# Attention preparation in four lanes instead of three, squares in PSUM, the root asked for in another place

## Chip, cores and metric

The kernel runs on 1 core of one Trainium2 chip. The metric is the device time in microseconds (us) of one execution. The engines are TensorE (PE; PEld is its weight loads), VectorE (DVE), ScalarE (ACT), GpSimd (POOL) and SyncE (SP), which issues most DMAs.

## What is computed

Two blocks in a row on 1024 tokens and 256 context tokens of width 1024. The first block has two layers with a multi-head latent attention (8 heads, 96 wide: 64 plain and 32 rotated), two convolution branches and an output product; the second block has scans and a mixture of 64 experts. What the change touches is the preparation of queries and keys in the first block:

```python
def mla_q(cq, q_norm_w, w_uq, q_head_norm_w, cos, sin):
    q = (rms_norm(cq, q_norm_w) @ w_uq).reshape(B, T, MLA_HEADS, MLA_QK)
    q = rms_norm(q, q_head_norm_w)
    if cos is not None:
        q = jnp.concatenate([q[..., :MLA_NOPE], apply_rope(q[..., MLA_NOPE:], cos, sin)], axis=-1)

def mla_kv(ckv, kr, kv_norm_w, w_ukv, k_head_norm_w, cos, sin):
    kv = (rms_norm(ckv, kv_norm_w) @ w_ukv).reshape(B, T, MLA_HEADS, MLA_NOPE + MLA_V)
    k_nope, v = kv[..., :MLA_NOPE], kv[..., MLA_NOPE:]
    k = rms_norm(jnp.concatenate([k_nope, k_rope], axis=-1), k_head_norm_w)
    ...
```

Keys are rotated as queries are; context tokens are not rotated. `rms_norm(x, w)` is `x * rsqrt(mean(x*x) + eps) * w`. All is float32.

## The kernel before, in words

The kernel is one hand-ordered program: each engine has its own queue, filled in program order, and semaphores tie them together. The first block's attention is in `attention(l, last)`, called once for each of the two layers. It has a preparation, then a gate (all engines wait until all is done and landed), then the attention proper (scores, softmax, products), which again ends the stage for everyone. So nothing of another stage runs beside the preparation, and nothing of the attention proper starts ahead of its end.

**The start of the preparation.** SyncE loads `cq`, `ckv`, `kr` and two weights. ScalarE squares `cq` and `ckv` (L1088, L1090). TensorE sums the squares with products against one column of ones (L1100, L1101), 30 of them in layer 0 and 26 in layer 1, all into bank 6. VectorE scales the weights (L1068, L1070) and lays the tables of the rotation (L1077, L1078), then turns the sums into variances (L1080, L1081); ScalarE takes the roots (L1092, L1093), VectorE the reciprocals (L1083, L1084): `rq` and `rkv`, one factor for each token.

**The rows.** A row is one tile of 128 tokens for the queries ("q") or for the keys and values ("k"). Layer 0 has 20 rows (10 tiles, q and k in turn), layer 1 has 18 (the two context tiles only as k). Row n goes through these steps:

- TensorE: the product into the two PSUM banks of its lane (L1118 for q: 8 matmul instructions, 384 columns wide; L1120 for k: 4, 512 wide). The bank must have been left by the last copy of the row that used the lane before (`out`).
- ScalarE: copies out of the banks into `qt_`, times `rq` or `rkv` (L1143, two for q; L1145 and L1146, four for k).
- ScalarE: squares of `qt_` into `sqt` (L1151, 768 elements a partition, in SBUF).
- VectorE: sum of the squares by head (L1176), times 1/96 plus eps (L1178).
- ScalarE: the root (L1154, 8 elements).
- VectorE: reciprocal (L1181), `qt_` times it (L1183, 768 elements), then the rotation: L1190, L1191, L1193, L1194, or only L1197 for the two context tiles. For a k row VectorE also lays the position part into `qt_` (L1173).
- TensorE: eight transposes into the same banks (L1129).
- ScalarE: two copies out into `QT` or `KTt` (L1161, `out`).

**The order of the queues.** Three lanes (`work`, lane n % 3) hold the rows in flight: `hs`, `qt_`, `sqt`, `tmpr` in SBUF, and two banks each. `staged` writes the queues: it walks time steps t, and at each step it lets every lane that has begun (row n begins at step 2n) go on to its next `yield`, the oldest first. So the number of `yield`s in `prep_tensor`, `prep_scalar` and `prep_vector` sets where an instruction stands in its engine's queue. In ScalarE's queue this gives, at step 2m: copies out of row m-2, root of row m-1, copies in of row m; at step 2m+1: squares of row m. In VectorE's: reciprocal and scaling of row m-1 and position of row m; then rotation of row m-1 and sums of row m. In TensorE's: transposes of row m-2, product of row m.

Of the kernel before, what the change touches and what calls it, by code (L numbers as in the profile page):

```python
# [9 lines left out]
ALU = mybir.AluOpType  # L10
# [259 lines left out]
def program(nc, A, B, out, ar, ps, sems, known, pe, dve, act, pool, sp):  # L270
# [744 lines left out]
    def attention(l, last):  # L1015
# [26 lines left out]
        assert o <= LIM, (o, LIM)  # L1042
# [20 lines left out]
        def vector(e):  # L1063
# [15 lines left out]
            e.wait_ge(*Tn.at("sums"))  # L1079
            e.tensor_scalar(rq[:, ti0:NT], bank(6)[:, ti0:NT], 1.0 / 256, 1e-6, ALU.mult, ALU.add).then_inc(Vn.hit(), 1)  # L1080
            e.tensor_scalar(rkv, bank(6)[:, 16:26], 1.0 / 128, 1e-6, ALU.mult, ALU.add).then_inc(Vn.hit("vars"), 1)  # L1081
            e.wait_ge(*Sn.at("roots"))
            e.reciprocal(rq[:, ti0:NT], rq[:, ti0:NT]).then_inc(Vn.hit(), 1)  # L1083
            e.reciprocal(rkv, rkv).then_inc(Vn.hit("scales"), 1)  # L1084

        def scalar(e):
# [4 lines left out]
            e.wait_ge(*Vn.at("vars"))  # L1091
            e.activation(rq[:, ti0:NT], rq[:, ti0:NT], ACT.Sqrt).then_inc(Sn.hit(), 1)  # L1092
            e.activation(rkv, rkv, ACT.Sqrt).then_inc(Sn.hit("roots"), 1)  # L1093

        def tensor(e):
            e.wait_ge(*Sn.at("squares"))
            for ti in range(NT):
                if P * ti >= c0:
                    for k in range(2):
                        e.matmul(bank(6)[:, ti:ti + 1], sqa[:, k, P * ti:P * ti + P], ones[:, 0:1], start=k == 0, stop=k == 1)  # L1100
                i = e.matmul(bank(6)[:, 16 + ti:17 + ti], sqa[:, 2, P * ti:P * ti + P], ones[:, 0:1], start=True, stop=True)  # L1101
            i.then_inc(Tn.hit("sums"), 1)

        sync(sp), vector(dve), scalar(act), tensor(pe)
        rows = [(ti, kind) for ti in range(NT) for kind in ("q", "k") if kind == "k" or P * ti >= c0]

        def prep_tensor(e, n):
# [3 lines left out]
            hs, tmpr, qt_, sqt, bk = work[n % 3]  # L1111
            e.wait_ge(*Vn.at("weights"))
            for g in range(2):
                if n >= 3:
                    e.wait_ge(*Sn.at("out", n - 3, g))
# [5 lines left out]
                op.then_inc(Tn.hit("mm", n, g), 1)  # L1121
            yield
# [2417 lines left out]
```

## Time and profile before

| | |
|---|---|
| median of 3 runs | 4926.18 us (4925.58 to 4941.12) |
| profiled execution | 4966.66 us, of it the span 4964.8 us |
| busy: TensorE / VectorE / ScalarE / GpSimd | 86% / 40% / 27% / 10% |
| preparation, layer 0 | from 497.46 to 622.66 us of the span |
| preparation, layer 1 | from 1511.87 to 1625.83 us of the span |

Each of these two stretches runs from the first square of the stage to the end of its last copy out. The shares of the first line of busy times are means over the whole program; what the change is worth is to be read in the two stretches. The column PEclk of the views by stretch is the clock that TensorE was granted: 0.50 is 1.2 GHz, 1.00 is 2.4 GHz.

### The profile page before, as it was taken

The page shows a single profiled execution, that of the slowest core. Times are in us where ns is not written, and L with a number is a line of the kernel's source. Part 1 is how long each engine was busy: PE and PEld are TensorE (multiplying, and loading weights), DVE is VectorE, ACT ScalarE, POOL GpSimd, SP SyncE. Part 2 cuts the span into 40 slices and gives each one's busy share as a digit, 9 for nine tenths or more (in the row PEclk, how much of TensorE's full clock was granted, in tenths as well). Part 3 has the DMA queues.
Part 4 walks back from the last instruction along what each step waited for, and adds up shares of the span by engine and source line. Part 5 has one row for each costly group of instructions (what it writes and reads, how often), then busy time and mean ns, then how long its engine had stood idle before and what let it go on. Part 6 is the DMA issues. An engine that isn't in the chain of part 4 may idle for free. (4 is left out here: it accounts for less than half of the span.)

```text
span 4964.8 us, 68829 instructions
## 1 busy us (share of the span) xinstructions
PE 4278.5 (86%) x28006; PEld 2476.6 (50%) x28006; DVE 2000.1 (40%) x4088; ACT 1344.0 (27%) x3101; POOL 517.7 (10%) x560
## 2 busy tenths in 40 slices
PE   5999799999997899999997745788788799999991
PEld 2454456644444565454556534677575344434340
DVE  1631556611714665221006667666355222222223
ACT  2111645511015554111014454333141111111111
POOL 0000000000000000000010001222003322322220
PEclk9999879999998999999997867998897899999995
DMA  5011000030110002412111030000303578999973
GB/s 187 21 61 53 18 18 14 18 140 20 56 52 33 14 14 104 172 48 72 43 64 39 1 99 1 3 3 3 110 1 144 215 253 289 310 332 337 333 254 123
DMA packets 152451, 505.37 MB, mean 102 GB/s; under 512 B 22609, under 2 KB 79554, under 8 KB 138690
## 3 DMA queue, kind: packets, MB, share of 16 engines
q1 hardware_dynamic: 114898, 379.89, 20.6%
q0 software_dynamic: 37232, 120.99, 8.8%
q8 instruction: 227, 3.72, 0.3%
q14 instruction: 94, 0.77, 0.1%
HBM read 402.42 MB, written 98.42 MB: 101 GB/s over the span
## 5 line engine op out<-in xcount | busy, mean ns | idle before, releaser
L697 PE MATMUL banks<-arena 128*128 128x512 f32 (+1 forms) x2928 | 1107.7, 540 | 16.1 <-DMA arena<-in_w_in 10.4
L697 PEld LDWEIGHTS banks<-arena 128*128 128x128 f32 x2928 | 559.0, 191 | 563.6 <-issue 522.8
L3125 PE MATMUL banks<-arena 128*32 128x512 f32 (+2 forms) x2896 | 561.2, 595 | 3.1 <-DMA arena<-in_experts 2.3
L884 PE MATMUL banks<-arena 128*128 128x256 f32 (+1 forms) x1152 | 379.9, 485 | 21.6 <-DMA arena<-y_d 14.3
L1248 PE MATMUL banks<-arena 96*128 96x512 f32 (+1 forms) x800 | 376.7, 554 | 11.8 <-ACT arena L1351 10.1
L3125 PEld LDWEIGHTS banks<-arena 128*32 128x32 f32 (+2 forms) x2896 | 198.4, 130 | 357.0 <-issue 354.3
L1298 DVE TENSOR_REDUCE arena<-banks 128x1 f32<-128x512 f32 (+1 forms) x400 | 238.1, 595 | 242.2 <-PE banks L1248 240.6
L884 PEld LDWEIGHTS banks<-arena 128*128 128x128 f32 x1152 | 223.2, 195 | 169.7 <-issue 149.8
L3144 PE MATMUL banks<-arena 128*32 128x512 f32 (+2 forms) x1448 | 286.4, 595 | 1.7 <-DVE arena L3174 1.2
L1256 PEld LDWEIGHTS banks<-arena 128*128 128x128 f32 x1312 | 171.4, 143 | 154.1 <-issue 123.3
L3092 POOL DMA_INDIRECT r_d<-arena x125 | 181.5, 1452 | 639.0 <-DVE arena L3174 531.5
L1351 ACT ACTIVATE arena<-banks,arena 128x512 f32<-128x512 f32 (+1 forms) x400 | 239.3, 606 | 16.0 <-DVE arena L1307 2.8
L3209 ACT ACTIVATE arena<-banks 128x256 f32<-128x256 f32 x79 | 30.4, 385 | 780.5 <-PE banks L3125 780.5
L3181 DVE SCALAR_TENSOR_TENSOR arena<-arena,banks 128x256 f32<-128x256 f32 x79 | 38.1, 482 | 493.6 <-ACT arena L3209 493.6
L1256 PE MATMUL banks<-arena 128*128 128x128 f32 x1312 | 213.6, 276 | 0.1
L1357 ACT ACTIVATE arena<-banks 128x256 f32<-128x256 f32 (+1 forms) x272 | 131.8, 484 | 288.9 <-PE banks L1256 288.7
L1269 PE MATMUL banks<-arena 128*64 128x128 f32 x2624 | 191.9, 283 | 17.5 <-DVE arena L1312 13.4
L896 DVE SCALAR_TENSOR_TENSOR arena<-banks,arena 128x256 f32<-128x256 f32 (+1 forms) x72 | 43.2, 600 | 375.5 <-PE banks L884 375.5
L715 ACT ACTIVATE arena<-banks 128x512 f32<-128x512 f32 (+1 forms) x94 | 51.4, 547 | 514.2 <-PE banks L697 514.2
L3174 DVE TENSOR_TENSOR arena<-banks,arena 128x1024 f32<-128x1024 f32 x79 | 96.8, 1226 | 225.5 <-PE banks L3144 225.5
L723 ACT ACTIVATE arena<-banks 128x512 f32<-128x512 f32 (+3 forms) x95 | 50.5, 532 | 465.6 <-PE banks L697 460.2
L804 DVE SCALAR_TENSOR_TENSOR arena<-arena 128x1296 f32<-128x1296 f32 (+1 forms) x120 | 171.2, 1427 | 4.3
(505 smaller groups left out, 5714.8 us busy)
## 6 DMA issues: line engine op xcount, KB each, us to landing
arena<-in_experts SPq DMA_DIRECT2D x64, 3072.0 KB, 12.9
arena<-in_ada_w SPq DMA_DIRECT2D x12, 2048.0 KB, 7.6
arena<-in_w_in SPq DMA_DIRECT2D x19, 1024.0 KB, 6.7
arena<-in_w_mod SPq DMA_DIRECT2D x8, 2048.0 KB, 18.3
arena<-in_w_in SPq DMA_DIRECT2D x7, 2048.0 KB, 9.3
arena<-in_w_out SPq DMA_DIRECT2D x6, 2048.0 KB, 13.0
arena<-in_w_mod SPq DMA_DIRECT2D x8, 1024.0 KB, 5.4
arena<-r_d SPq DMA_DIRECT2D x16, 512.0 KB, 5.4
```

The lines of the kernel that those rows point to most:

```text
L697: i = e.matmul(self.out_of(n), lhs, rhs, start=k == 0, stop=k == KT - 1)
L804: e.scalar_tensor_tensor(z[:, lo:hi], a[:, lo - 15 + j:hi - 15 + j], reg(cw + 2 * j + ft, 1), z[:, lo:hi], ALU.mult, ALU.add).then_inc(Vn. ...
L884: i = e.matmul(bank(n % 4)[:, 0:nn], w[:, q, :], H[:, q, t0:t0 + nn], start=q == 0, stop=q == KT - 1)
L1248: op = e.matmul(bank(q)[:, 0:P * jn], QT[:, h, P * ti:P * ti + P], KTt[:, h, P * j0:P * (j0 + jn)], start=True, stop=True)
L1256: op = e.transpose(bank(3 + q)[:, P * j:P * j + P], pr[n % 2][:, P * (j0 + j):P * (j0 + j) + P], ident)
L1269: op = e.matmul(b[64 * (h % 2):64 * (h % 2) + 64, 0:P], V[:, j, 64 * h:64 * h + 64], ptr[n % 4][:, P * j:P * j + P], start=j == 0, stop=j ...
L1298: e.tensor_reduce(c[:, q:q + 1], bank(q)[:, 0:P * jn], AX.X, ALU.max).then_inc(Vn.hit(), 1)
L1351: e.activation(pr[n % 2][:, P * j0:P * (j0 + jn)], bank(q)[:, 0:P * jn], ACT.Exp, bias=c[:, 3:4], scale=SM, accum_out=c[:, 4 + q:5 + q]).t ...
L1357: e.activation(ptr[n % 4][:, P * j0:P * (j0 + jn)], bank(3 + q)[:, 0:P * jn], ACT.Copy).then_inc(Sn.hit("turn", n, q), 1)
L3092: e.indirect_dma_start(r_d[i % 2], bass.IndirectOffsetOnAxis(ap=lists[rows.start][0:rows.stop - rows.start, q, 0:1].bitcast(U32), axis=0), ...
L3125: op = e.matmul(ABK[(q - q0) % 2][rows, :], xT[(q - q0) % 2][:, P * k:P * k + P][:, rows], weights[:, i % SLOTS, 512 * k:512 * k + 512], s ...
L3144: op = e.matmul(OBK[rows, 512 * n:512 * n + 512], hT[(q - q0) % 2][:, P * f:P * f + P][:, rows], weights[:, i % SLOTS, o:o + 512], start=f ...
```

## The change

Four lanes instead of three, each with two of the eight banks. Room for the fourth lane: the squares no longer have a place in SBUF but go into the first 384 columns of the lane's two banks (`squares`), from which the row's copies have been made by then, and the two halves of `tmpr` lie apart. The sum over each head (now L1197) reads PSUM. The token sums at the start are split into two groups of tiles (0 to 2 into bank 6, 3 to 9 into bank 7); the second group's work is written behind the product of row 0. In the rows, the root is one `yield` later, the copies out are one or two later, and VectorE's rotation follows the scaling without a `yield`. Cut to its core:

```diff
-        for i in range(3):
+        for i in range(4):
             hs = reg(o, 8); o += 8
             qt_ = reg(o, 768).rearrange("p (h n) -> p h n", h=HN); o += 768
-            sqt = reg(o, 768).rearrange("p (h n) -> p h n", h=HN)
-            tmpr = reg(o, 512).rearrange("p (a h n) -> p a h n", a=2, h=HN); o += 768
-            work.append((hs, tmpr, qt_, sqt, [bank(2 * i), bank(2 * i + 1)]))
+            tmpr = [reg(at, 256).rearrange("p (h n) -> p h n", h=HN) for at in (o, o + 256 if i < 3 else ST + 3840)]; o += 512 if i < 3 else 256
+            squares = ps[:, 1024 * i:1024 * i + 1024].rearrange("p (g n) -> p g n", g=2)[:, :, 0:384]
+            work.append((hs, tmpr, qt_, squares, [bank(2 * i), bank(2 * i + 1)]))
...
+        groups = [(0, 3, bank(6)), (3, NT, bank(7))]
+
+        def sums_tensor(e, g):
+            t0, t1, out = groups[g]
             e.wait_ge(*Sn.at("squares"))
+            for ti in range(t0, t1):
+                if ti >= ti0:
                     for k in range(2):
+                        op = e.matmul(out[:, ti:ti + 1], sqa[:, k, P * ti:P * ti + P], ones[:, 0:1], start=k == 0, stop=k == 1)
+                op = e.matmul(out[:, 16 + ti:17 + ti], sqa[:, 2, P * ti:P * ti + P], ones[:, 0:1], start=True, stop=True)
+            op.then_inc(Tn.hit("sums", g), 1)
+            yield
...
+        steps(sums_tensor(pe, 0)), steps(sums_vector(dve, 0)), steps(sums_scalar(act, 0))
...
         def prep_tensor(e, n):
...
-                if n >= 3:
-                    e.wait_ge(*Sn.at("out", n - 3, g))
+                if n >= 4:
+                    e.wait_ge(*Sn.at("out", n - 4, g))
+                elif n == 3:
+                    e.wait_ge(*Vn.at("vars", 1))
...
             yield
             yield
             yield
+            yield
             e.wait_ge(*Vn.at("turned", n))
...
         def prep_scalar(e, n):
...
             yield
-            e.wait_ge(*Sn.at("rows", n))
+            e.wait_ge(*Sn.own())
             if kind == "k":
                 e.wait_ge(*Vn.at("position", n))
-            e.activation(sqt, qt_, ACT.Square).then_inc(Sn.hit("sq", n), 1)
+            e.activation(squares, qt_.rearrange("p h n -> p (h n)").rearrange("p (g n) -> p g n", g=2), ACT.Square).then_inc(Sn.hit("sq", n), 1)
+            yield
             yield
             e.wait_ge(*Vn.at("var", n))
             e.activation(hs, hs, ACT.Sqrt).then_inc(Sn.hit("root", n), 1)
+            yield
             yield
             yield
             if n < 2:
...
         def prep_vector(e, n):
...
             e.wait_ge(*Sn.at("sq", n))
-            e.tensor_reduce(hs, sqt, AX.X, ALU.add).then_inc(Vn.hit(), 1)
+            e.tensor_reduce(hs.rearrange("p (g h) -> p g h", g=2), squares.rearrange("p g (h n) -> p g h n", h=4), AX.X, ALU.add).then_inc(Vn.hit(), 1)
             e.wait_ge(*Vn.own())
             e.tensor_scalar(hs, hs, 1.0 / QK, 1e-6, ALU.mult, ALU.add).then_inc(Vn.hit("var", n), 1)
+            yield
             yield
             e.wait_ge(*Sn.at("root", n))
             e.reciprocal(hs, hs).then_inc(Vn.hit(), 1)
             e.wait_ge(*Vn.own())
             e.tensor_tensor(qt_, qt_, hs.unsqueeze(2).broadcast_to([P, HN, QK]), ALU.mult).then_inc(Vn.hit("scaled", n), 1)
-            yield
             w32, cw, sw = turns[kind]
...
+        for e, lane, sums in ((pe, prep_tensor, sums_tensor), (dve, prep_vector, sums_vector), (act, prep_scalar, sums_scalar)):
+            staged((1, sums(e, 1)), *((2 * n, lane(e, n)) for n in range(len(rows))))
```

Two places show what this does to the queues. The first is ScalarE's queue in the rows of layer 0, from the copies out of an old row on; L1161 and, in the changed kernel, L1182 are copies out, L1154 and L1174 the root, L1143 and L1162 the copies in of a q row, L1145/L1146 and L1164/L1165 those of a k row, L1151 and L1170 the squares. Before:

```order
L1161 ACTIVATE arena<-banks,arena 96x4x128 x2
L1154 ACTIVATE arena<-arena 128x8
L1143 ACTIVATE arena<-banks,arena 128x384 x2
L1151 ACTIVATE arena<-arena 128x768
L1161 ACTIVATE arena<-banks,arena 96x4x128 x2
L1154 ACTIVATE arena<-arena 128x8
L1145 ACTIVATE arena<-banks,arena 128x4x64
L1146 ACTIVATE arena<-banks,arena 128x256
L1145 ACTIVATE arena<-banks,arena 128x4x64
L1146 ACTIVATE arena<-banks,arena 128x256
L1151 ACTIVATE arena<-arena 128x768
```

and the same place of the changed kernel:

```order
L1182 ACTIVATE arena<-banks,arena 96x4x128 x2
L1162 ACTIVATE arena<-banks,arena 128x384 x2
L1174 ACTIVATE arena<-arena 128x8
L1170 ACTIVATE banks<-arena 128x2x384
L1182 ACTIVATE arena<-banks,arena 96x4x128 x2
L1164 ACTIVATE arena<-banks,arena 128x4x64
L1165 ACTIVATE arena<-banks,arena 128x256
L1164 ACTIVATE arena<-banks,arena 128x4x64
L1165 ACTIVATE arena<-banks,arena 128x256
L1174 ACTIVATE arena<-arena 128x8
L1170 ACTIVATE banks<-arena 128x2x384
```

The root stood behind the copies out and ahead of the copies in; now it stands behind the copies in of the next row and right ahead of that row's squares, and the copies out belong to a row one further back.

The second is VectorE's queue around one row with rotation (L1183 and L1205 the scaling, L1176 and L1197 the sums of squares, L1173 and L1194 the position). Before, from the variance of one row to that of the next:

```order
L1178 TENSOR_SCALAR arena<-arena 128x8
L1181 RECIPROCAL arena<-arena 128x8
L1183 TENSOR_TENSOR arena<-arena 128x768
L1173 COPY arena<-arena 128x8x32
L1190 TENSOR_TENSOR arena<-arena 128x256
L1191 TENSOR_TENSOR arena<-arena 128x256
L1193 TENSOR_TENSOR arena<-arena 128x8x16
L1194 TENSOR_TENSOR arena<-arena 128x8x16
L1176 TENSOR_REDUCE arena<-arena 128x8
L1178 TENSOR_SCALAR arena<-arena 128x8
```

and the same place of the changed kernel:

```order
L1199 TENSOR_SCALAR arena<-arena 128x8
L1194 COPY arena<-arena 128x8x32
L1203 RECIPROCAL arena<-arena 128x8
L1205 TENSOR_TENSOR arena<-arena 128x768
L1211 TENSOR_TENSOR arena<-arena 128x256
L1212 TENSOR_TENSOR arena<-arena 128x256
L1214 TENSOR_TENSOR arena<-arena 128x8x16
L1215 TENSOR_TENSOR arena<-arena 128x8x16
L1197 TENSOR_REDUCE arena<-banks 128x8
L1199 TENSOR_SCALAR arena<-arena 128x8
```

The position copy moved ahead of the reciprocal, and the sums read the banks; the rest keeps its order. In TensorE's queue the product of row m now stands ahead of the transposes of row m-2, and in layer 0 21 of the 30 token sums stand behind the product of row 0.

## Rows read from the trace of the kernel before

**Rows 1.** Busy by stretch: length, PE, PEld, DVE, ACT, POOL, PEclk, DMA share, GB/s:

```profile
497.46:622.66 125.20, 89.22 (x340) 57.93 (x340) 71.97 (x173) 76.11 (x145) 0.00 (x0) 0.81 0.05 15
1511.87:1625.83 113.96, 81.36 (x300) 52.20 (x300) 66.57 (x163) 69.10 (x133) 0.00 (x0) 0.80 0.05 16
```

**Rows 2.** Waits from 520 to 620 us (us in total, times, longest):

```profile
PE banks L1129 <- DVE arena L1194: 23.1, 11, 3.0
...
DVE arena L1176 <- ACT arena L1151: 19.9, 12, 5.5
...
DVE arena L1181 <- ACT arena L1154: 14.9, 20, 1.8
```

**Rows 3.** Timeline in layer 0 (start us, us, engine, line, operation):

```profile
570.87 0.17 DVE L1178 TENSOR_SCALAR arena<-arena 128x8 f32<-128x8 f32 x1
571.08 0.21 ACT L1154 ACTIVATE arena<-arena 128x8 f32<-128x8 f32 x1
571.19 0.46 ACT L1145 ACTIVATE arena<-banks,arena 128x256 f32<-128x256 f32 x1
...
572.43 0.28 DVE L1173 COPY arena<-arena 128x256 f32<-128x256 f32 x1
...
572.81 0.84 ACT L1151 ACTIVATE arena<-arena 128x768 f32<-128x768 f32 x1
...
574.65 1.26 ACT L1161 ACTIVATE arena<-banks,arena 96x512 f32<-96x512 f32 x2 [1.00 <-PE banks L1129]
...
574.81 0.17 DVE L1178 TENSOR_SCALAR arena<-arena 128x8 f32<-128x8 f32 x1
...
575.81 0.20 ACT L1154 ACTIVATE arena<-arena 128x8 f32<-128x8 f32 x1
```

**Rows 4.** Roots by layer (first and last start), and two of them in the timeline:

```profile
L1154 ACT ACTIVATE arena<-arena x20: 196/202/211, 521.7 to 617.2; 128x8 f32<-128x8 f32 x20
...
L1154 ACT ACTIVATE arena<-arena x18: 195/201/210, 1532.8 to 1620.4; 128x8 f32<-128x8 f32 x18
...
538.49 0.21 ACT L1154 ACTIVATE arena<-arena 128x8 f32<-128x8 f32 x1
...
1542.86 0.21 ACT L1154 ACTIVATE arena<-arena 128x8 f32<-128x8 f32 x1
```

**Rows 5.** Timeline, products and transposes on TensorE:

```profile
513.89 5.05 PE L1118 MATMUL banks<-arena 128*128 128x384 f32 x8
...
563.32 1.94 PE L1129 MATMUL banks<-arena 128*96 128x128 f32 x8 [2.90 <-DVE arena L1194]
...
573.97 1.08 PE L1129 MATMUL banks<-arena 128*96 128x128 f32 x8 [2.48 <-DVE arena L1194]
574.89 2.75 PE L1118 MATMUL banks<-arena 128*128 128x384 f32 x8
...
1526.16 6.65 PE L1120 MATMUL banks<-arena 128*128 128x512 f32 x8
```

**Rows 6.** Busy time by stretch in layer 0 (PEclk is third from the end):

```profile
520.00:541.00 21.00, 13.58 (x58) 7.49 (x56) 14.40 (x30) 16.91 (x35) 0.00 (x0) 1.00 0.00 1
...
541.00:616.00 75.00, 54.22 (x203) 32.75 (x204) 51.11 (x123) 49.96 (x100) 0.00 (x0) 0.87 0.00 1
...
563.00:566.00 3.00, 2.69 (x10) 2.32 (x11) 1.29 (x4) 1.39 (x3) 0.00 (x0) 0.50 0.00 0
```

**Rows 7.** Groups by shape, whole span, VectorE: sums of 512, 256 and 768 elements:

```profile
L1298 DVE TENSOR_REDUCE arena<-banks 128x1 f32<-128x512 f32 x256 | 177.0, 691 | 212.6 <-PE banks L1248 211.1
...
L1298 DVE TENSOR_REDUCE arena<-banks 128x1 f32<-128x256 f32 x144 | 61.1, 424 | 29.6 <-PE banks L1248 29.6
...
L1176 DVE TENSOR_REDUCE arena<-arena 128x8 f32<-128x768 f32 x38 | 36.1, 949 | 36.6 <-ACT arena L1151 36.6
```

**Rows 8.** Layer 1: token sums on TensorE, and the last weight scaling:

```profile
L1101 PE MATMUL banks<-arena x20: 341/352/352, 1515.1 to 1526.0; 128*128 128x1 f32 x20
...
1517.43 0.75 DVE L1070 TENSOR_SCALAR arena<-arena 128x1024 f32<-128x1024 f32 x1 [0.17 <-DMA arena<-in_w_ukv]
```

More of the change, by code:

```diff
@@ new lines, in sums_tensor, with sums_vector @@
+                op = e.matmul(out[:, 16 + ti:17 + ti], sqa[:, 2, P * ti:P * ti + P], ones[:, 0:1], start=True, stop=True)
+            op.then_inc(Tn.hit("sums", g), 1)
+            yield
+        def sums_vector(e, g):
+            t0, t1, out = groups[g]
+            q0 = max(t0, ti0)
+            e.wait_ge(*Tn.at("sums", g))
+            e.tensor_scalar(rq[:, q0:t1], out[:, q0:t1], 1.0 / 256, 1e-6, ALU.mult, ALU.add).then_inc(Vn.hit(), 1)
+            e.tensor_scalar(rkv[:, t0:t1], out[:, 16 + t0:16 + t1], 1.0 / 128, 1e-6, ALU.mult, ALU.add).then_inc(Vn.hit("vars", g), 1)
+            e.wait_ge(*Sn.at("roots", g))
+            e.reciprocal(rq[:, q0:t1], rq[:, q0:t1]).then_inc(Vn.hit(), 1)
+            e.reciprocal(rkv[:, t0:t1], rkv[:, t0:t1]).then_inc(Vn.hit("scales", g), 1)
+            yield
@@ L1105, in attention, with sums_scalar @@
+        def sums_scalar(e, g):
+            t0, t1, out = groups[g]
+            q0 = max(t0, ti0)
+            e.wait_ge(*Vn.at("vars", g))
+            e.activation(rq[:, q0:t1], rq[:, q0:t1], ACT.Sqrt).then_inc(Sn.hit(), 1)
+            e.activation(rkv[:, t0:t1], rkv[:, t0:t1], ACT.Sqrt).then_inc(Sn.hit("roots", g), 1)
+            yield
+        sync(sp), vector(dve), scalar(act)
+        steps(sums_tensor(pe, 0)), steps(sums_vector(dve, 0)), steps(sums_scalar(act, 0))
         rows = [(ti, kind) for ti in range(NT) for kind in ("q", "k") if kind == "k" or P * ti >= c0]
@@ L1110, in prep_tensor @@
             tok = slice(P * ti, P * ti + P)
[L1111 removed]
+            hs, tmpr, qt_, squares, bk = work[n % 4]
             e.wait_ge(*Vn.at("weights"))
             for g in range(2):
[L1114 to L1115 removed]
+                if n >= 4:
+                    e.wait_ge(*Sn.at("out", n - 4, g))
+                elif n == 3:
+                    e.wait_ge(*Vn.at("vars", 1))
                 if kind == "q":
@@ L1135, in prep_scalar @@
             ti, kind = rows[n]
-            hs, tmpr, qt_, sqt, bk = work[n % 3]
+            hs, tmpr, qt_, squares, bk = work[n % 4]
             dst = QT if kind == "q" else KTt
-            e.wait_ge(*Vn.at("scales"))
+            e.wait_ge(*Vn.at("scales", int(ti >= 3)))
             for g in range(2):
@@ L1166, in prep_vector @@
             ti, kind = rows[n]
-            hs, tmpr, qt_, sqt, bk = work[n % 3]
+            hs, tmpr, qt_, squares, bk = work[n % 4]
             if kind == "k":
@@ L1199, in prep_vector @@
             yield
-        for e, lane in ((pe, prep_tensor), (dve, prep_vector), (act, prep_scalar)):
-            staged(*((2 * n, lane(e, n)) for n in range(len(rows))))
+        for e, lane, sums in ((pe, prep_tensor, sums_tensor), (dve, prep_vector, sums_vector), (act, prep_scalar, sums_scalar)):
+            staged((1, sums(e, 1)), *((2 * n, lane(e, n)) for n in range(len(rows))))
         gate()
```

26 lines of the change are left out of this document (6 added, 20 removed).

## The prediction

> **What bounds the kernel now.** I began with the page. Its busy times are means over many stages, and the change is in two of them only, so I asked for the busy time of those two stretches. The preparations take 125.2 and 114.0 us, 239 us in all, 4.8% of the span, and no engine fills them: in layer 0 TensorE is busy 89 us, VectorE 72 and ScalarE 76 of 125 [rows 1]. A stretch in which three engines are each busy for 57 to 71% is bound by a chain that passes from one to the other, not by an engine.
>
> The waits say where it passes [rows 2]. From 520 to 620 us VectorE waited 19.9 us for squares (L1151) and 14.9 us for roots (L1154), and TensorE 23.1 us for rotated rows (L1194). The timeline shows why the root is late [rows 3]. At 574.81 VectorE starts the variance of a row; 0.21 us after such a start a free ScalarE can take the root (570.87 to 571.08). But ScalarE has just begun the two copies out, at 574.65, and its root starts at 575.81: 1.0 us after the variance instead of 0.21. The squares are late for the other reason: they stand behind copies in that wait for a product, and the product stands in TensorE's queue behind the transposes of an older row, which wait for its rotation. So rotation, product, copies in, squares and sums of different rows make one ring. The result is 5.25 us for a row in layer 0 (538.49 to 617.2 for 15 rows) and 5.17 in layer 1 (1542.86 to 1620.4) [rows 4].
>
> 0.3% of the time, 14.8 us, is about what a measurement of this kernel can tell from no change.
>
> **The rows with rotation.** In the new queue of ScalarE the root of a row comes after the copies out of an old row and the copies in of the next one, and all this lies beside VectorE's work on the row ahead. So I lay both loops out from one root to the next.
>
> VectorE: from the root at 571.08 through reciprocal, scaling, position, rotation and sums to the start of the next variance at 574.81 is 3.73 us, plus 0.21 to the next root: 3.94 [rows 3]. The position copy now stands ahead of the reciprocal, where VectorE waits for the root anyway. Taken out of the chain it gives back only about 0.1: it takes about 0.2 us of the queue, but the first product of the rotation waits for the end of the scaling in any case. That leaves 3.85 us.
>
> ScalarE, for a k row, the longer kind (four copies in against two): two copies out and on to the next instruction 1.16 (574.65 to 575.81), copies in 1.62 (571.19 to 572.81), the root 0.11 (571.08 to 571.19), squares 0.84: 3.73 us [rows 3]. Less than 3.85, so VectorE is the bound, with 0.12 us to spare in k rows and more in q rows. The product now stands ahead of those transposes, so the ring is cut: with the copies in waiting for nobody, the squares are ready when VectorE comes for them, which ends the 19.9 us, and the root is asked for when ScalarE stands idle at it, which ends most of the 14.9 us.
>
> TensorE at its full clock: transposes 0.92 for each row (573.97 to 574.89), a q product 2.75, a k product about 1.7 (half of half of the 6.65 us that two k rows took at 1.2 GHz): 6.3 us for a pair of rows, against 7.7 for VectorE's loop [rows 5]. It has cover as long as the clock stays up. The new wait of a product, for the copies out of row n-4, costs nothing: those copies stand one row earlier in ScalarE's queue than the copies in that need the product. Behind a waiting product stand the transposes of row n-2; VectorE finishes them only later, so nobody is held up.
>
> 15 periods in layer 0: 15 x (5.25 - 3.85) = 21.0 us. 15 in layer 1: 15 x (5.17 - 3.85) = 19.8 us.
>
> **Squares in PSUM.** No row shows ScalarE writing PSUM, nor VectorE summing 768 elements from it. For the sums, the nearest rows: 256 elements from the banks take 424 ns and 512 take 691, so another 256 should make 958, against 949 from SBUF now [rows 7]. 9 ns for each of 38 rows is 0.3 us, which I take as nothing; twice the time is the far end, and stands below as a rival. For the write, a gain is possible and would be hidden. An added cost is hidden up to the 0.12 us that ScalarE has to spare in a k row. The square in SBUF takes 0.84 us [rows 3]; if it took a third more, 0.28, each of the 20 k rows would be 0.16 us late, 3 us in all. I take 0, as the shape is the same, and keep the 3 us. The Trainium skill ("VectorE: DVE Perf Modes", the errata section with the cycle table) gives a PSUM source 120 cycles of fixed cost against 58 for SBUF. By that the sum would be an estimated 65 ns dearer for each row, some 2 us in all. The rows of 512 and 768 elements do not show it, and the measurement decides.
>
> **The early rows and the start.** In layer 0 TensorE has the same work ahead of the product of row 1 as before (30 token sums and the product of row 0, only in another order), so the copies of row 1, and the first root right behind them, come at the same time: 0. From there to the root at 538.49 four rows took 16.8 us [rows 4]. Without rotation VectorE's loop is about 1 us shorter, 2.85, and ScalarE's is 3.73 for k and less for q; I take the middle, 3.3, thus 13.2 us and a gain of 3.6, and keep 1.9 to 5.4.
>
> In layer 1 splitting the sums costs something. All 26 took 11.1 us, from 1515.1 to 1526.16 [rows 5, 8]. The first five now end near 1517.2, but the product of row 0 needs the weights, whose scaling ends at 1518.2 [rows 8]: TensorE idles 1.0 us, and the product of row 1, after the other 21 sums, comes that much later. Then the first root waits for the copies in of row 1 and the second for those of row 2, a q product. Against that stand two rows at a shorter period. I take a gain of 1.0 us up to the root at 1542.86, and keep -1 to +3.
>
> **The tail** (last root to last copy out) is the same chain as before: 0. If TensorE should still be at its full clock there, each transpose group is 0.86 us shorter (1.94 against 1.08) [rows 5]; that is for the range. Every engine passes the gate, so what the stage gains, the kernel gains, and no DMA starts earlier into anything.
>
> **The sum.** Layer 0: 21.0 + 3.6 = 24.6. Layer 1: 19.8 + 1.0 = 20.8. In all 45.4 us. The profiled execution (4966.66 us, span 4964.8) would come to 4921.3; it stood 40 us above the median, and carrying the difference over to the median, 4926.18 - 45.4 = 4880.8 us, 0.92% faster.
>
> **Rivals.** (1) *TensorE's clock goes on falling as often as now.* It was at 1.00 from 520 to 541 us, and 0.87 on average from 541 to 616, a quarter of that time at 1.2 GHz [rows 6]. It fell after TensorE had stood idle for 2.90 us at 563.32, waiting for the rotation [rows 5], with 0.50 in the three us from 563 [rows 6]. At 1.2 GHz a pair of rows costs TensorE twice 1.6 for transposes, 5.05 for the q product and 3.3 for the k product, 11.6 us, 5.8 a row. If a quarter of the 30 periods still ran so, 7.5 x (5.8 - 3.85) = 15 us come back: 4896. Against it: the new loop leaves TensorE idle for 1.4 us in 7.7, never for 2.9 at once. 10%.
>
> (2) *The sums from PSUM are much dearer in this form* (two banks, a pattern of four dimensions). If a sum took twice its 0.95 us, the loop would be 4.8: 30 periods and two tails x 0.95 = 30 us come back and 4911 is left. The rows of sums speak against it [rows 7]. 3%.
>
> (3) *Slower: TensorE becomes the bound at half clock.* The token sums have 1 column and ran at the low clock; now 21 of them stand between the first products, and the new order puts the root behind copies in that wait for a product. If the clock never rose, every row would cost 5.8 us against 5.2 before: 30 x 0.6 = 18 us lost, and 4 x (5.8 - 4.2) = 6 in the early rows, 4950 us. Between 45 gained at the full clock and 24 lost at the low one it decides from the point where two thirds of the rows run at 1.2 GHz. Against it: at 513.89 the clock was at 1.2 GHz (a q product of 5.05 us against 2.75), TensorE ran without a pause, and from 520 on it had 1.00 [rows 5, 6]; a TensorE that is the bound never pauses. 3%. The Trainium skill ("TensorE: Matmul & The Clock Gate", part 1) says that sustained activity releases the throttle and idling brings it back; by that rule this rival undoes itself, and the trace agrees in the stretch from 513.89 to 541.
>
> (4) *The change doesn't do what it says*: ScalarE, not VectorE, turns out to be the loop's bound, because the copies in still wait for products, and the root with them. Then the period stays midway, at 4.5 between 3.85 and 5.2; 30 x 0.65 = 20 us come back, and 4900 is left. For it: the root has more in front of it than before. Against it: a product needs only copies out that stand a row ahead. 4%.
>
> **How the numbers follow.** Forecast 80%, rivals 10, 3, 3 and 4%. The predicted time is the forecast's own, 4880.8. Its own bounds: below, 1.8 and 2 more in the early rows, 1.5 at the tails and 3 if handovers are shorter, about 8 us, to 4872; above, 1.7 and 2 at the start, 3 for PSUM and 4 if they are longer, about 11, to 4892. The range reaches down to 4868, since the three runs before differ by 15 us, and up to 4904, which takes in (1) and (4). Faster by over 0.3% means under 4911.4: the forecast, (1) and (4), less a little for a disturbed median, 0.93. Within 0.3%: (2), on the edge, and that little, 0.04. Slower: (3), 0.03.
>
> **What would show it.** In the new profile: preparations of about 101 and 93 us; roots 3.85 us apart in the rows with rotation; VectorE busy for over 85% of the time in these rows, its waits for the squares near 0 and for the root about 0.25 us each; TensorE's clock at 1.00 there; the sum from the banks at 950 to 960 ns. I am wrong if the roots are over 4.2 us apart, if ScalarE never waits for the variance (L1199), if TensorE still waits 2 us and more for the rotation, or if the stage after the gate changes its time.

## The result, and the profile after

| | before | changed |
|---|---|---|
| median | 4930.06 us (4925.58 to 4941.12, 6 runs) | 4890.99 us (4876.53 to 4897.8, 6 runs) |
| profiled execution | 4966.66 us | 4883.45 us |
| preparation, layer 0 | 125.20 us | 99.73 us |
| preparation, layer 1 | 113.96 us | 93.81 us |

The ratio on record is 0.9904 with a 95% interval of 0.9888 to 0.992, that is 39 to 55 us less and clearly outside 0.3%. It is not the ratio of the two medians in the table, which differ by 39 us (0.9921), at the edge of that interval. The prediction was 4880.8 us, a ratio of 0.9908 to its own 4926.18; the median of 4890.99 lies in its range of 4868 to 4904.

The two preparations together are 45.6 us shorter; the prediction's sum was 45.4. The two profiled executions differ by 83 us, though. What remains, 38 us, lies in stages that the change does not touch, above all in the last one, after layer 1's preparation: 3338.97 us before, 3295.62 after. A second profiled execution of the changed kernel (run 10 below) took 3325.4 us for the same stretch (from 1569.8 to 4895.2), and run 8, whose later stages are those of the changed kernel too, 3343.1. The stretch scatters by more than 40 us from one execution to the next, so those 43 us can't be put down to the change; nor can a smaller effect of it on that stretch be ruled out. This is why I read the two stages and not the difference of two whole profiles.

The busy time by stretch of the changed kernel, the two preparations, columns as in [rows 1]:

```profile
499.39:599.12 99.73, 81.04 (x340) 51.75 (x340) 72.30 (x177) 72.74 (x147) 0.00 (x0) 0.86 0.06 18
1492.17:1585.98 93.81, 74.75 (x300) 47.52 (x300) 67.00 (x167) 66.39 (x135) 0.00 (x0) 0.83 0.06 20
```

VectorE is busy for the same 72 us as before, in 100 us instead of 125. The waits in the rows with rotation of layer 0 (540 to 594 us; waiting engine and line, releaser, us in total, times, longest):

```profile
PE banks L1148 <- DVE arena L1215: 11.6, 14, 2.8
ACT arena L1174 <- DVE arena L1199: 7.9, 14, 1.6
DVE arena L1203 <- ACT arena L1174: 1.9, 7, 0.3
```

The wait of VectorE for the squares, 19.9 us in [rows 2], is not in the list any more. Its wait for the root is 1.9 us in 14 rows where it was 14.9 in 20. In its place stands a new one, of ScalarE for the variance (7.9 us): now ScalarE stands at the root ahead of time, in all 14 rows. TensorE still waits for the rotation, but for 0.8 us at a time in the mean, 0.21 and 1.07 by turns. The longest wait, 2.8 us, stands where no product is left to be done, ahead of the last transposes but one:

```profile
592.58 1.94 PE L1148 MATMUL banks<-arena 128*96 128x128 f32 x8 [2.79 <-DVE arena L1215]
```

The roots, first and last of each layer, as in [rows 4], and the timeline of one row of the changed kernel, from one root to the next:

```profile
L1174 ACT ACTIVATE arena<-arena x20: 201/209/218, 522.3 to 593.6; 128x8 f32<-128x8 f32 x20
L1174 ACT ACTIVATE arena<-arena x18: 201/210/218, 1515.5 to 1580.5; 128x8 f32<-128x8 f32 x18
```

```profile
562.44 0.17 DVE L1199 TENSOR_SCALAR arena<-arena 128x8 f32<-128x8 f32 x1
562.51 1.88 PE L1138 MATMUL banks<-arena 128*128 128x512 f32 x4
562.65 0.21 ACT L1174 ACTIVATE arena<-arena 128x8 f32<-128x8 f32 x1 [0.64 <-DVE arena L1199]
562.76 0.80 ACT L1170 ACTIVATE banks<-arena 128x768 f32<-128x768 f32 x1
562.89 0.20 DVE L1203 RECIPROCAL arena<-arena 128x8 f32<-128x8 f32 x1 [0.28 <-ACT arena L1174]
563.13 0.96 DVE L1205 TENSOR_TENSOR arena<-arena 128x768 f32<-128x768 f32 x1
563.50 1.24 ACT L1182 ACTIVATE arena<-banks,arena 96x512 f32<-96x512 f32 x2
564.12 0.43 DVE L1211 TENSOR_TENSOR arena<-arena 128x256 f32<-128x256 f32 x1
...
564.64 0.46 ACT L1164 ACTIVATE arena<-banks,arena 128x256 f32<-128x256 f32 x1
...
565.33 0.95 DVE L1197 TENSOR_REDUCE arena<-banks 128x8 f32<-128x768 f32 x1
...
566.31 0.17 DVE L1199 TENSOR_SCALAR arena<-arena 128x8 f32<-128x8 f32 x1
...
566.39 0.29 DVE L1194 COPY arena<-arena 128x256 f32<-128x256 f32 x1
566.52 0.21 ACT L1174 ACTIVATE arena<-arena 128x8 f32<-128x8 f32 x1 [0.34 <-DVE arena L1199]
```

From root to root it is 3.87 us (562.65 to 566.52), and every row is alike: 3.87 us on average over 15 rows, in layer 0 as in layer 1. VectorE's instructions follow each other from 562.89 to 566.39 without a wait. The copies in (564.64) follow the copies out at once. Their product runs from 562.51 on, ahead of them. The position copy (566.39) lies in the time in which the root is on its way. Before, the copies in of a q row waited for their product, 13.9 us in all from 520 to 620 us:

```profile
ACT arena L1143 <- PE banks L1118: 13.9, 17, 1.8
```

The two instructions that now touch PSUM, by group over the whole span, the sums and the squares (mean ns behind the comma), and the squares of the kernel before:

```profile
L1197 DVE TENSOR_REDUCE arena<-banks 128x8 f32<-128x768 f32 x38 | 36.2, 952 | 7.7 <-ACT banks L1170 7.7
```

```profile
L1170 ACT ACTIVATE banks<-arena 128x768 f32<-128x768 f32 x38 | 30.7, 808 | 0.7
```

```profile
L1151 ACT ACTIVATE arena<-arena 128x768 f32<-128x768 f32 x38 | 32.1, 844 | 1.6
```

A sum of 768 elements from the banks takes 952 ns against 949 from SBUF [rows 7], and a square is 36 ns shorter when it writes PSUM.

### The profile page after: what moved, and what is told of

Same layout as the page of the kernel before. It is cut to its first block and busy times, and to the rows that moved or that the text cites. A ratio compares the mean times of both kernels' runs of the same rounds, so it can differ in the third digit from the quotient of the medians.

```text
span 4881.6 us, 68841 instructions
## 1 busy us (share of the span) xinstructions
PE 4242.7 (87%) x28006; PEld 2450.6 (50%) x28006; DVE 2002.0 (41%) x4096; ACT 1338.1 (27%) x3105; POOL 518.7 (11%) x560
## 5 line engine op out<-in xcount | busy, mean ns | idle before, releaser
L1372 ACT ACTIVATE arena<-banks,arena 128x512 f32<-128x512 f32 (+1 forms) x400 | 239.3, 606 | 16.1 <-DVE arena L1328 2.9
```

The lines of the kernel that those rows point to most:

```text
L1372: e.activation(pr[n % 2][:, P * j0:P * (j0 + jn)], bank(q)[:, 0:P * jn], ACT.Exp, bias=c[:, 3:4], scale=SM, accum_out=c[:, 4 + q:5 + q]).t ...
```

## The experiments

My theory when they were designed, the "ring": before, the rows waited for each other in a circle (rotation, transposes and product behind it in TensorE's queue, copies in, squares, sums, rotation). The product ahead of the transposes and the fourth lane cut it, and VectorE's own work is the new bound. The rivals: the lanes alone did it, the order alone, the place of the root, the squares in PSUM, the split of the token sums, or TensorE's clock.

All that follows is read from one profiled execution of each kernel. "Prep." is from the first square of the stage to the end of the last copy out; "period" is the mean distance of roots from the fifth root on in layer 0 and from the third on in layer 1; the clock is PEclk from about 540 us to layer 0's last root. The whole times of single runs scatter by 15 us and more, so they decide nothing of a few us. The preparation of layer 1 scatters too: 93.8 and 90.3 us in two executions of the changed kernel, all of it ahead of the third root.

| kernel | prep. 0 / 1, us | period 0 / 1, us | clock |
|---|---|---|---|
| before | 125.2 / 114.0 | 5.25 / 5.17 | 0.87 |
| changed | 99.7 / 93.8 | 3.87 / 3.87 | 0.98 |
| 1 before, squares in PSUM | 125.4 / 112.5 | 5.25 / 5.09 | 0.87 |
| 2 four lanes, old order | 117.9 / 110.3 | 5.03 / 5.24 | 0.91 |
| 3 three lanes, new order | 115.1 / 103.4 | 4.67 / 4.67 | 1.00 |
| 4 before, TensorE kept busy | 117.0 / 104.4 | 4.69 / 4.69 | 1.00 |
| 5 transposes ahead of the product | 177.3 / 165.8 | 8.17 / 8.27 | 0.76 |
| 6 root a step earlier | 99.2 / 91.9 | 3.87 / 3.87 | 0.99 |
| 7 token sums in one group | 100.8 / 90.8 | 3.87 / 3.87 | 0.98 |
| 8 sums of squares twice | 117.3 / 106.7 | 4.86 / 4.86 | 0.94 |
| 9 squares twice | 104.3 / 94.4 | 4.06 / 4.06 | 0.98 |
| 10 changed, once more | 100.0 / 90.3 | 3.87 / 3.87 | 0.98 |
| 11 rotation a step later | 100.2 / 89.8 | 3.76 / 3.78 | 1.00 |
| 12 as 11, one group in layer 1 | 100.3 / 89.8 | 3.76 / 3.76 | 1.00 |

**1. The squares in PSUM alone,** in the kernel before:

```diff
-            e.activation(sqt, qt_, ACT.Square).then_inc(Sn.hit("sq", n), 1)
+            e.activation(squares, qt_.rearrange("p h n -> p (h n)").rearrange("p (g n) -> p g n", g=2), ACT.Square).then_inc(Sn.hit("sq", n), 1)
...
-            e.tensor_reduce(hs, sqt, AX.X, ALU.add).then_inc(Vn.hit(), 1)
+            e.tensor_reduce(hs.rearrange("p (g h) -> p g h", g=2), squares.rearrange("p g (h n) -> p g h n", h=4), AX.X, ALU.add).then_inc(Vn.hit(), 1)
```

> The kernel before (three lanes, old order), with its squares in PSUM and the sums read from there; nothing else changes. Ring theory (rotation, product, copies in, squares and sums of different rows wait for each other because of the order of TensorE's queue): the place of the squares is no part of the gain, preparations of 125 and 114 us within 2. Theory that PSUM squares are what helped (808 ns instead of 844 and less waiting): 3 us and more shorter in each layer.

125.4 and 112.5 us: 1.3 us in all, which is within the scatter of layer 1. The place of the squares is no part of the gain; what it gives is room for a lane.

**2. Four lanes, with the queues in the old order.** The changed kernel (so with the squares in PSUM and the token sums split) with these yields:

```diff
@@ prep_tensor, between product and transposes
-            yield
@@ prep_scalar, between squares and root
-            yield
@@ prep_scalar, between root and copies out
-            yield
@@ prep_vector, between variance and reciprocal
-            yield
@@ prep_vector, between scaling and rotation
+            yield
```

> The changed kernel with four lanes, but with the old order of all three queues (transposes four steps behind the product, root and reciprocal at step 2, copies out at step 4, rotation a step behind the scaling). Ring theory: the order makes the wait and the fourth lane gives next to nothing: roots still about 5.2 us apart, preparations of 121 to 125 and 110 to 114 us. Buffer theory (a product had to wait for its two banks): roots under 4.2 us apart, preparations near 100 and 94.

Layer 0 is 7.3 us shorter than before, layer 1 3.6. I had expected 0 to 4 us less in each, so layer 0 is better than I thought, but far from the 100 and 94 of the buffer theory. The waits of layer 0 (540 to 600 us) are of the kind of before, with the products and the transposes on the same ring:

```profile
PE banks L1147 <- DVE arena L1212: 17.4, 11, 2.9
DVE arena L1199 <- ACT arena L1172: 9.7, 12, 1.8
ACT arena L1179 <- PE banks L1147: 8.5, 13, 1.5
ACT arena L1161 <- PE banks L1136: 8.3, 12, 1.6
```

Where this run's gain lies says more than its size. 8.8 of the 10.9 us come ahead of the fifth root in layer 0 and of the third in layer 1; the rows behind them take 3.3 us less in layer 0 and 1.1 us more in layer 1. And where TensorE's clock is at 1.00, the distance between roots is that of the kernel before, to 0.01 us: 4.65 and 4.72 here, 4.64 and 4.73 there (571.08 to 575.81 in [rows 3], then to 580.45). Three roots of this run, and the stretch around them:

```profile
586.12 0.20 ACT L1172 ACTIVATE arena<-arena 128x8 f32<-128x8 f32 x1
590.84 0.20 ACT L1172 ACTIVATE arena<-arena 128x8 f32<-128x8 f32 x1
595.49 0.20 ACT L1172 ACTIVATE arena<-arena 128x8 f32<-128x8 f32 x1
```

```profile
577.00:595.00 18.00, 11.60 (x55) 7.11 (x54) 13.93 (x33) 13.38 (x27) 0.00 (x0) 1.00 0.00 1
```

So in the old order the fourth lane takes nothing off a row; the periods of 5.03 and 5.24 differ from 5.25 and 5.17 by how many rows ran below the full clock.

**3. Three lanes, with the queues in the new order:**

```diff
-        for i in range(4):
+        for i in range(3):
...
-                if n >= 4:
-                    e.wait_ge(*Sn.at("out", n - 4, g))
-                elif n == 3:
-                    e.wait_ge(*Vn.at("vars", 1))
+                if n >= 3:
+                    e.wait_ge(*Sn.at("out", n - 3, g))
...
```

> The changed kernel with three lanes, order as changed. A product then waits for the copies out that stand right ahead of its own copies in on ScalarE, so ScalarE sees the whole product: outs 1.16, wait and copies some 2.4 to 3.2, root and squares 0.86: about 4.5 us a row. Ring theory with buffers as the second half: preparations of about 113 and 104 us, so the order alone brings about half of the 45 us. If the order alone were the gain: 100 and 94. If the lanes alone were it: 125 and 114.

115.1 and 103.4 us, the roots 4.67 us apart: near what was expected, somewhat under half of the gain. The timeline shows the wait that the fourth lane takes away; a product begins only when the copies out (L1180) leave its bank, and the copies in (L1160) wait for it:

```profile
560.02 2.82 PE L1134 MATMUL banks<-arena 128*128 128x384 f32 x8 [1.60 <-ACT arena L1180]
...
561.65 0.58 ACT L1160 ACTIVATE arena<-banks,arena 128x384 f32<-128x384 f32 x1 [1.20 <-PE banks L1134]
...
562.88 0.58 ACT L1160 ACTIVATE arena<-banks,arena 128x384 f32<-128x384 f32 x1 [0.65 <-PE banks L1134]
563.36 0.20 ACT L1172 ACTIVATE arena<-arena 128x8 f32<-128x8 f32 x1
...
563.59 0.20 DVE L1201 RECIPROCAL arena<-arena 128x8 f32<-128x8 f32 x1 [1.43 <-ACT arena L1172]
```

The root at 563.36 stands behind both copies in, so VectorE waits 1.43 us for it. Run 2 gave 10.9 us, this run 20.7, both halves together 45.6: each half removes a wait that the other leaves standing.

Of these 20.7 us, 16.1 lie in the rows. But here the clock was at 1.00 in the rows with rotation, up to the last row of layer 1, where the kernel before had 0.87 on average, and the roots come 5.04 and 4.42 us apart by turns, 4.73 in the mean, no less than the 4.69 of the old order at the full clock (run 4). So what the order alone took off the rows is what the fallen clock had cost. Only order and fourth lane together take a row well under 4.69 us at the same clock.

**4. The kernel before, with TensorE kept busy** in its idle time ahead of the transposes of q rows:

```diff
             yield
             yield
+            if kind == "q":
+                if n == 0:
+                    e.wait_ge(*Vn.at("vars"))
+                for k in range(2):
+                    e.matmul(bank(7), cq[:, k, tok], wq[:, k, 0:512], start=True, stop=True)
             e.wait_ge(*Vn.at("turned", n))
```

> The kernel before, with two matmuls of 512 columns into an unused bank put ahead of the transposes of every q row, where TensorE stands idle for 2.5 to 3 us; their output is never read. If the falling clock made part of the old time: TensorE's clock stays at 1.00 in the rows, roots about 4.7 us apart, preparations of about 117 and 107 us. If the clock never mattered, because TensorE was not on the ring: 125 and 114 or more. If the extra 1.7 us of matmuls fall on the ring: over 125.

117.0 and 104.4 us with the roots 4.69 us apart. The stretch of the rows with rotation in this kernel, and the one of the kernel before for comparison:

```profile
540.00:610.00 70.00, 59.73 (x236) 32.71 (x234) 53.13 (x127) 52.98 (x106) 0.00 (x0) 1.00 0.00 1
```

```profile
540.00:617.00 77.00, 54.80 (x204) 32.90 (x204) 52.07 (x126) 51.71 (x102) 0.00 (x0) 0.87 0.00 1
```

More work on TensorE, and 17.8 us less in the two stages: so much of the old time goes with the clock's fall to 1.2 GHz, with the old ring still in place. The ring itself, at 2.4 GHz throughout, is 4.69 us a row.

**5. The transposes ahead of the product again,** four lanes and all else as changed:

```diff
@@ prep_tensor, between product and transposes
-            yield
```

> The changed kernel with one yield taken out of TensorE's lane: the transposes of row m-2 stand ahead of the product of row m again, four lanes and all else as changed. Ring theory: the product then waits for the rotation of row m-2, the copies in for the product, the root for the copies in and the next rotation for the root. From rotation to rotation: 0.34 + 0.9 + product 1.8 or 2.8 + copies 0.5 to 0.7 + root 0.24 + scaling and rotation 2.4, thus 6.2 to 7.1 us a row, preparations of about 150 and 137 us, worse than before the change. If TensorE's order were of no weight: 100 and 94.

177.3 and 165.8 us, 52 us worse in each layer than before the change, and worse than my 150 and 137. The timeline of one row; L1147 are the transposes, L1138 the product, L1163 the first copy in, L1173 the root:

```profile
575.59 1.94 PE L1147 MATMUL banks<-arena 128*96 128x128 f32 x8 [3.32 <-DVE arena L1214]
...
577.33 3.62 PE L1138 MATMUL banks<-arena 128*128 128x512 f32 x4
579.34 0.48 ACT L1163 ACTIVATE arena<-banks,arena 128x256 f32<-128x256 f32 x1 [4.43 <-PE banks L1138]
...
581.71 0.21 ACT L1173 ACTIVATE arena<-arena 128x8 f32<-128x8 f32 x1
...
581.95 0.20 DVE L1202 RECIPROCAL arena<-arena 128x8 f32<-128x8 f32 x1 [5.15 <-ACT arena L1173]
```

The ring stands there link by link: rotation, transposes, product, copies in, root, and VectorE idle for 5.15 us. My estimate took every product and transpose at the full clock. Here the transposes take 1.94 us where they took 1.08 at the full clock, and the product 3.62 where it took 1.88, 2.6 us more for a row; TensorE had stood idle for 3.32 us ahead of them, and the clock was at 0.76 on average:

```profile
540.00:670.00 130.00, 75.59 (x219) 42.98 (x218) 55.64 (x132) 54.94 (x112) 0.00 (x0) 0.76 0.00 0
```

**6. The root a step earlier** on ScalarE, ahead of the copies in:

```diff
@@ prep_scalar, between squares and root
-            yield
@@ prep_scalar, between root and copies out
+            yield
```

> The changed kernel with the root one step earlier in ScalarE's queue (behind the copies out, ahead of the copies in, as before the change); VectorE's and TensorE's queues as changed. VectorE bound: the place of the root is no part of the gain, since VectorE asks for it only after the next variance: roots 3.87 us apart, preparations within 1.5 us of 99.7 and 93.8. If the place of the root is what the gain rests on: roots 4.2 us and more apart, preparations 6 us longer each and more.

99.2 and 91.9 us, the period 3.87 us again. With the ring cut, the row takes the same time with the root in either place. The part of the change that its name speaks of gives nothing by itself here.

**7. The token sums in one group,** ahead of everything:

```diff
-        groups = [(0, 3, bank(6)), (3, NT, bank(7))]
+        groups = [(0, NT, bank(6))]
...
-            staged((1, sums(e, 1)), *((2 * n, lane(e, n)) for n in range(len(rows))))
+            staged(*((2 * n, lane(e, n)) for n in range(len(rows))))
```

> The changed kernel with the token sums in one group ahead of everything, as before. My account of the start: nothing but TensorE's idle time of 0.91 us in layer 1 hangs on the split, so layer 1 is 0 to 1 us shorter than 93.8 and layer 0 within 1 us of 99.7. If the split is a real part of the gain (row 0 starts 7 us earlier): both 3 us longer and more.

100.8 and 90.8 us. Layer 0 is 1.1 us longer, a little outside what I had expected, and layer 1 3.0 us shorter where I had said 0 to 1. But run 10, the changed kernel once more, took 90.3 us in layer 1 with the split in place, so those 3.0 us cannot be put down to it. The scatter is in the start of layer 1. In the first profile of the changed kernel the last 21 token sums ran like this:

```profile
1503.27 0.99 PE L1095 MATMUL banks<-arena 128*128 128x1 f32 x4
1504.12 0.56 PE L1096 MATMUL banks<-arena 128*128 128x1 f32 x2
```

and in run 10 like this:

```profile
1490.32 0.58 PE L1095 MATMUL banks<-arena 128*128 128x1 f32 x4
1490.77 0.36 PE L1096 MATMUL banks<-arena 128*128 128x1 f32 x2
```

Three sums in 1.28 us or in 0.67: in run 10 the clock rose behind the product of row 0 and was up for most of the sums; in the other execution it did not rise behind the same product (0.50 from 1503 to 1511 us), and why is open. The same kernel differs by 3.5 us there. That the split gains or costs anything was not shown.

**8. The sums of squares twice,** 0.95 us more on VectorE for each row:

```diff
+            e.tensor_reduce(hs.rearrange("p (g h) -> p g h", g=2), squares.rearrange("p g (h n) -> p g h n", h=4), AX.X, ALU.add).then_inc(Vn.hit(), 1)
+            e.wait_ge(*Vn.own())
             e.tensor_reduce(hs.rearrange("p (g h) -> p g h", g=2), squares.rearrange("p g (h n) -> p g h n", h=4), AX.X, ALU.add).then_inc(Vn.hit(), 1)
```

> The changed kernel with the sum of squares on VectorE made twice for every row (0.95 us and its wait, about 1.0). VectorE bound: roots 4.87 us apart instead of 3.87 and preparations of about 118 and 110 us, 1.0 us for each of the later rows. If ScalarE or TensorE were the bound with VectorE hidden: less than 0.5 us a row, under 110 and 104.

The roots are 4.865 us apart, 0.99 more than 3.873: all of the added time shows. VectorE is the bound.

**9. The squares twice,** 0.81 us and a wait more on ScalarE for each row:

```diff
+            e.activation(squares, qt_.rearrange("p h n -> p (h n)").rearrange("p (g n) -> p g n", g=2), ACT.Square).then_inc(Sn.hit(), 1)
+            e.wait_ge(*Sn.own())
             e.activation(squares, qt_.rearrange("p h n -> p (h n)").rearrange("p (g n) -> p g n", g=2), ACT.Square).then_inc(Sn.hit("sq", n), 1)
```

> The changed kernel with ScalarE's squares of each row made twice (0.81 us and the wait between them). VectorE bound with ScalarE close behind: a k row's loop on ScalarE goes from about 3.5 to 4.4 us and a q row's from about 3.0 to 3.9, so the roots go from 3.87 to about 4.15 us apart, preparations of about 106 and 99 us: a third of what the same time cost on VectorE. If ScalarE were the bound: roots 4.75 us apart.

4.06 us, 0.19 more, under a quarter of what was added, and less than I expected. The mean hides two kinds of row:

```profile
560.19 0.22 ACT L1176 ACTIVATE arena<-arena 128x8 f32<-128x8 f32 x1
564.08 0.21 ACT L1176 ACTIVATE arena<-arena 128x8 f32<-128x8 f32 x1
568.34 0.22 ACT L1176 ACTIVATE arena<-arena 128x8 f32<-128x8 f32 x1
```

Where a q row is copied in, the roots stay 3.88 to 3.89 us apart; where a k row is, they are 4.26 apart, and ScalarE has no wait left. The second square and its wait add 0.85 us to ScalarE, so in the changed kernel it has about 0.46 us to spare at a k row (3.87 + 0.85 - 4.26) and over 0.85 at a q row. ScalarE is not the bound, but close behind.

**10 to 12. The changed kernel once more, and two attempts to do better.** In run 11 the rotation follows the sums of the next row, so that it covers the way of the root to ScalarE and back; the transposes and the copies out come later accordingly:

```diff
@@ prep_tensor, between product and transposes
+            yield
+            yield
@@ prep_scalar, between root and copies out
+            yield
@@ prep_vector, between scaling and rotation
+            yield
```

> The changed kernel itself, to be compared on the same chip with the two below. Preparations of 99.7 and 93.8 us, 39 to 47 us under the kernel before.

> The changed kernel with the rotation one step later on VectorE (it then stands behind the sums and the variance of the next row, so that it covers the way to ScalarE and back for the root), and the transposes and copies out later accordingly. VectorE bound with 0.25 us of waiting for the root in each row: roots about 3.63 us apart, preparations of about 98 and 91.5 us, 3 to 5 us under the changed kernel in all, near what this can resolve. If later transposes cost more than the cover gives: roots at 3.87 or more.

Run 12 adds to it, for layer 1 alone, one group of token sums:

```diff
-        groups = [(0, 3, bank(6)), (3, NT, bank(7))]
+        groups = [(0, NT, bank(6))] if last else [(0, 3, bank(6)), (3, NT, bank(7))]
```

> As the one with the later rotation, and the token sums of layer 1 again in one group ahead of everything (in layer 0 split as changed). Layer 0 about 98 us, layer 1 about 89: 6 to 7 us under the changed kernel in all. If the two edits get in each other's way: as the one with the later rotation alone.

Ratios to the kernel before: 0.9908 (0.9891 to 0.9924) for the changed kernel, which repeats the first measurement; 0.9886 (0.9864 to 0.9908) for run 11; 0.9893 (0.9876 to 0.9911) for run 12. The intervals overlap: neither is shown to be faster. The stages say the same: 100.2 and 89.8 us against 100.0 and 90.3. The period did fall, but to 3.76 us and not to 3.63. The timeline of run 11 shows what took VectorE's place:

```profile
561.65 1.25 ACT L1185 ACTIVATE arena<-banks,arena 96x512 f32<-96x512 f32 x2
...
562.79 0.20 ACT L1176 ACTIVATE arena<-arena 128x8 f32<-128x8 f32 x1
562.89 0.81 ACT L1172 ACTIVATE banks<-arena 128x768 f32<-128x768 f32 x1
563.02 0.20 DVE L1206 RECIPROCAL arena<-arena 128x8 f32<-128x8 f32 x1 [0.66 <-ACT arena L1176]
...
566.78 0.82 ACT L1172 ACTIVATE banks<-arena 128x768 f32<-128x768 f32 x1 [0.25 <-DVE arena L1197]
...
568.86 0.58 ACT L1164 ACTIVATE arena<-banks,arena 128x384 f32<-128x384 f32 x1 [0.65 <-PE banks L1136]
```

ScalarE now runs without a stop but for two short waits (0.25 for the position copy, which slid behind the rotation, and 0.65 for the second half of a q product), and VectorE waits 0.66 for its root every second row. And what the shorter periods save, 15 x 0.11 = 1.6 us in layer 0, is lost at the ends: from the last root (592.0) to the end of the last copy out (598.3) it takes 6.3 us, where the changed kernel takes 5.5, and the early rows come 1.3 us later.

## Why the prediction was right, point by point

**The bound.** Right: "one ring" of rotation, product, copies in, squares and sums. Runs 2, 3 and 5 show its two closures, TensorE's order and the lane's banks, and run 5 that one yield is enough to bring it back. The prediction gave the fourth lane no share of its own and put the whole cut down to the product's place ahead of the transposes; that was its gap. With the new order but three lanes the period is 4.67, not 3.87, and at the same clock that is no better than the old order (run 4, 4.69). The prediction also took the old 5.25 and 5.17 us as the ring's own; about 0.5 us of each was the fallen clock.

**The period.** 3.85 us forecast, 3.87 measured, in both layers. The chain that I read off one row of the old trace was VectorE's own work plus the way for one root, and it holds; run 8 shows that it is the bound. 15 x (5.25 - 3.87) + 15 x (5.17 - 3.87) = 40 us, where I had 40.8. ScalarE, for which I had 3.73 us at a k row and 0.12 to spare, has more room than that: by run 9 about 0.46 us at a k row. No run adds work to TensorE in the changed kernel, so what it has to spare is known only from its waits of 0.21 and 1.07 us.

**The early rows and the start.** Layer 0: four rows from 522.27 to 535.53, 13.3 us against 13.2 forecast. The first root came 22.9 us after the stage's first square, where it was 24.2 before, 1.3 us better than "at the same time". Layer 1: from the first square to the third root 30.2 us against 31.0 before, 0.8 us less where I took 1.0. Run 10 took 26.7 for the same, a gain of 4.3, so this term has a scatter of 3.5 us, nearly all of it at the token sums, where the clock differed; my bounds of -1 to +3 were too narrow.

**PSUM.** Right to cost it at nothing: 952 ns for a sum, 3 more than from SBUF and 6 less than the 958 that the rows of 256 and 512 elements gave. By the Trainium skill ("VectorE: DVE Perf Modes", the errata section with the cycle table) it would have been an estimated 65 ns more; neither the rows before nor the change show it. The write was 36 ns cheaper, and hidden, as was said.

**The tail.** The clock was at 1.2 GHz again for the last transposes (1.94 us each), as before. Layer 0's tail went from 5.5 to 5.5 us: nothing, as forecast.

**The rivals.** (1), the clock falling as often as now, did not come: 0.98 against 0.87. Run 4 puts a price on what it took away, 17.8 us of the old 239; the steady terms of the sum had this inside the measured 5.25 and 5.17. (2) and (4) fell with 952 ns and with the waits of ScalarE for the variance. (3) had the right mechanism, a root behind copies in that wait for a product, and run 5 shows that it can cost more than I gave it, 104 us over the kernel before and not 24; only it is TensorE's order that decides it, not the clock at the start.

**The signs.** VectorE was busy for 92% of the time from 540 us to the last root of layer 0 (49.49 of 53.64 us), its waits for the root were 0.3 us at most, and the clock was at 1.00 from 540 to 590 us, all as forecast. Two of the signs of being wrong need a word. TensorE's wait for the rotation is over 2 us once in each layer, in the last rows, where no product is left, and nowhere else. And the stage after the gate did change its time, by 43 us between the two profiled executions; since it differs by up to 48 us between executions with the same later stages (3295.6 and, in run 8, 3343.1), this sign could not be read at all.

**The total.** 45.4 us forecast, 45.6 in the two stages, 39 between the medians (a ratio of 0.9921), and 0.9904 on record against 0.9908 forecast. That the two stages agree to 0.2 us is partly luck: with run 10 in place of the first profile they are 48.9 us shorter. The median is 10 us over the forecast; 4 of them are the median of before, which moved from 4926 to 4930 with more runs, and the other 6 are inside the scatter of 21 us of the changed kernel's own runs.

## What to carry to other kernels

Where three engines are each busy for 60% and wait for each other, write down for each engine what stands behind what in its queue, and look for a closed ring; then see what one instruction moved across another opens. Buffers and order are one question: at the full clock a row took 4.69 us before, 4.69 with the fourth lane alone, 4.73 with the order alone, and 3.87 with both. Compare such times only at the same granted clock, or the clock's share is taken for the change's: the order alone seemed to give 21 us. And the new period could here be read off the old trace, as the longest chain of one engine's own work with one handover, to within 1%: 3.85 us read, 3.87 measured.

## What the runs showed of the hardware

- In the kernel before, two matmuls of no use for every q row, some 1.9 us each time, put where TensorE had stood idle, made the two stages 17.8 us shorter; the granted clock stayed at 1.00 where it had been 0.87.
- The clock can be low, and fall, while TensorE is busy without a pause. The kernel before ran 11 us of products against one column at 0.50 (1.2 GHz) in layer 1. In run 10 the clock had risen behind the product of row 0; it was granted 0.87 from 1489 to 1493 us and 0.61 from 1493 to 1495, with TensorE busy for all of it with such products, and three sums went from 0.67 us back to 1.28.
- A square of 768 elements that writes PSUM took 808 ns, one that writes SBUF 844.
